# One head a step in stick-breaking, index projections later, a sixteenth weight slot, in a two-block transformer kernel

## The chip, the cores and the metric

The kernel runs on one core of a Trainium2 chip. The metric is the device time of one execution in microseconds. The engines are TensorE (PE), VectorE (DVE), ScalarE (ACT), GpSimd (POOL) and SyncE (SP, which issues most transfers). Each has its own program, written out by hand; semaphores join them.

## The reference

Two transformer blocks on 512 tokens of 1024 features in float32. Block one has two layers. Its first layer mixes with eight heads of "fox" attention (softmax with a cumulative forget gate) and eight heads of DSA (a small index score picks the keys), its second with NSA; each is followed by an MLP. Block two has four heads of differential attention, eight heads of stick-breaking attention, and a mixture of 32 experts. The parts that the change touches, cut down:

```python
def dsa_mixer(...):                       # block one, layer one
    q_abs = einsum('bshe,rhe->bshr', q[..., ROPE_DIM:], w_uk)
    rel = relu(einsum('bqhd,bsd->bqhs', qi, k_idx))      # index score
    score = einsum('bqhs,bqh->bqs', rel, wi)
    ...                                   # top 128 keys, softmax over them
    return einsum('bshr,rhd->bshd', o_lat, w_uv)

def fox_mixer(q, k, v, f_logit):
    cum = cumsum(log_sigmoid(f_logit))
    logits = q @ k.T * scale + cum_q - cum_k
    ...

def stick_breaking(q, k, v):              # block two, 8 heads of 64
    z = q @ k.T * scale
    log_1m = where(causal, log_sigmoid(-z), 0.0)
    between = cumsum(log_1m, reverse=True) - log_1m
    a = where(causal, exp(log_sigmoid(z) + between), 0.0)
    return a @ v                          # then rms_norm per head, then w_o

def hier_moe(h, ...):                     # top 2 of 8 experts in the top group
    for each expert e:
        ys = (silu(xb @ w1[e]) * (xb @ w3[e])) @ w2[e]
    return sum over the two experts of gate * ys
```

## The kernel before

Activations lie transposed, features on the 128 partitions and the 512 tokens along the free dimension. Dense layers go through `pe_block`, a scheme of seven products instead of eight on two blocks at a time, with six weight tiles in a ring. Two PSUM banks (`ch6`, `ch7`) are channels for small results: PE fills one, ACT or DVE takes it to SBUF (`act_take`, `dve_take`), and PE waits until it has been emptied. The stages come one after another, and four of them matter here.

**Preparation, index and soft steps (block one).** `pe_ab_prepare` rotates and turns queries and keys. At its end it projects the shared latent (`ck`, two tiles) to the DSA keys (`k_dsa`, four tiles, L627 and L628) and values (`v_dsa`, four tiles, L633). `dve_ab_prepare` forms the forget gates' cumulative sums, takes half of those tiles, and builds the operands `fls` and `frs` that add a gate to the logits (L1657 to L1663). Then `pe_index` computes the index scores (L653), which DVE adds up (L1681). After it run sixteen fox steps and sixteen DSA steps, each a pair of heads and a block of 128 queries (`pe_soft`), software-pipelined over PE, ACT and DVE. SP brings the gates' rows into `frs` and `fls` by sixteen small transfers, and writes the rows of the relative-position bias out (`row`), while the soft steps run.

**Stick-breaking (block two).** `pe_sb`, `act_sb` and `dve_sb` run over four pairs of heads. The score matrix of a head is kept by key blocks j, so that block j has the 512 - 128 j queries at or after it; `PARTS` lists the eight blocks of a pair:

```python
PARTS = [(a, j, T - P * j) for a in range(2) for j in range(NB - 1, -1, -1)]
```

For each block PE forms logits (L974), ACT scales them out of PSUM (L1356), DVE masks the diagonal (L1976) and forms -|z| (L1981), ACT takes exp and ln(1 + .) (L1361, L1366), DVE adds max(z, 0) (L1996). So softplus(z) is there. PE sums it over later keys with a triangular and a ones matrix (L984, L986), DVE subtracts (L1985), ACT takes exp (L1370), and PE forms the values with the weights stationary (L994, twenty matmuls of 64 columns for a pair; the trace records each matmul of the program as two, so x40). DVE takes these, PE turns them (L1000), ACT takes them again. The banks are reused within a pair, and no pair begins its later sums before its logits are done. When all pairs are done, eight tiles `u` are normalised (`pe_norm_tiles` L881, `act_norm_tiles` L1071, L1079 and L1081, `dve_norm_tiles` L1921), and the output projection 2O begins.

**Experts.** 32 experts of six weight pieces of 1 MiB each. SP issues the 192 loads in the order `ORDER` into `SLOTS` = 15 places (L2150); a place is free when PE has used its piece (`w_used`). Eight of the places are free before the dense layers end, since the others lie over tiles that are still in use:

```python
if g == SLOTS - LATE:
    sp.wait_ge(s["prod_done"], 7 * N_CH // 2)
```

Each expert handles up to 64 tokens: POOL gathers them from `h_tokens` and scatters the result into `y_pairs`, DVE forms the indices (`dve_slots`, `dve_indices`) two experts ahead, PE runs the up matmuls (L2285) and the down matmuls (L2293). The last three experts are added by PE and DVE without going through memory (`pe_last` L2354, `dve_last` L2506). At the end SP loads the four blocks of `y_pairs` (1 MiB each, L2184), DVE adds them to the tokens `xtok` (L2491, L2493), and four transfers write the output. `pe_tokens` turns `x` into `xtok` around expert 0.

## Time and profile before

| what | value |
|---|---|
| median of 3 runs | 2469.31 us (2463.83 to 2474.63) |
| the profiled execution, its own time | 2470.12 us |
| its span | 2468.7 us |
| PE busy | 2286.4 us, 93% |
| DVE busy | 1391.5 us, 56% |
| ACT busy | 566.9 us, 23% |
| POOL busy | 65.9 us, 3% |
| data moved | 350.18 MB |

The span is the part of an execution between the first and the last recorded instruction; the own time of the same execution is 1.4 us longer. Busy shares are means over stages that have different limits, so each stage has to be read by itself. A row of a stretch gives start and end, its length, then for PE, PE's weight loads, DVE, ACT and POOL the busy time and the number of instructions, then PE's granted clock (1.00 is 2.4 GHz, 0.50 is 1.2 GHz), the DMA engines' busy share and GB/s.

### The profile page before, as it was taken

How to read it: one execution, taken by the hardware profiler on the slowest of the kernel's cores; microseconds unless marked ns; L12 is line 12 of the kernel's file. 1: busy time of each engine (PE TensorE's matmuls, PEld its weight loads, DVE VectorE, ACT ScalarE, POOL GpSimd, SP SyncE). 2: the span in 40 equal slices, each digit the busy share in tenths (PEclk: the TensorE clock that was granted, in tenths of full speed). 3: DMA queues.
4: the chain of work that ended last, by engine and by line, in shares of the span. 5: the costliest groups of instructions: out<-in, count | busy, mean ns of one | idle time of the engine just before them, and what ended most of it. 6: DMA issues, size and time to landing. Idle time of an engine off the chain costs nothing.

```text
span 2468.7 us, 29460 instructions
## 1 busy us (share of the span) xinstructions
PE 2286.4 (93%) x10906; PEld 1674.5 (68%) x10906; DVE 1391.5 (56%) x3563; ACT 566.9 (23%) x1397; POOL 65.9 (3%) x67
## 2 busy tenths in 40 slices
PE   8987889999999988999999999999889899898887
PEld 6863668888888876557888888887566733333332
DVE  6558857666566555997665666765756411111114
ACT  2013342101001013773110011202554211211111
POOL 0000000000000000000000000000000011111110
PEclk9998799999999986999999999999799898999999
DMA  5320022222222420001222332322003699999996
GB/s 204 92 60 7 11 75 83 88 86 86 86 86 86 157 69 0 1 2 52 86 86 92 90 91 86 103 86 68 1 1 130 243 388 419 419 419 419 420 420 279
DMA packets 69455, 350.18 MB, mean 142 GB/s; under 512 B 10804, under 2 KB 11060, under 8 KB 43776
## 3 DMA queue, kind: packets, MB, share of 16 engines
q1 hardware_dynamic: 64144, 339.18, 37.4%
q0 software_dynamic: 4880, 8.05, 0.9%
q8 instruction: 89, 1.46, 0.3%
q10 hardware_dynamic: 288, 1.05, 0.1%
q14 instruction: 54, 0.44, 0.1%
HBM read 343.05 MB, written 17.30 MB: 146 GB/s over the span
## 4 chain that ended last, share of the span: by engine, by line
PE 68%; DVE 7%; DMA 7%; ACT 3%; issue 2%; SPq 0%; DVEq 0%; POOLq 0%; ACTq 0%
PE bank L550 25%; PE bank L563 7%; PE bank L553 7%; PE bank L558 7%; DMA w<-in_experts 6%; PE bank L2285 6%; PE bank L2293 4%; PE bank L541 2%; DVE exps L1695 1%; PE bank L767 1%; PE bank L2261 1%; PE bank L812 1%; PE bank L837 1%; DMA y_pairs<-oN,idx 1%; PE bank L825 1%
## 5 line engine op out<-in xcount | busy, mean ns | idle before, releaser
L2285 PE MATMUL bank<-w,xT 128*64 128x512 f32 x1024 | 228.3, 594 | 8.1 <-DMA w<-in_experts 7.4
L2464 DVE COPY square<-bank 128x256 f32<-128x256 f32 x32 | 13.6, 425 | 356.8 <-ACT rope L2384 356.8
L2285 PEld LDWEIGHTS bank<-w,xT 128*64 128x64 f32 x1024 | 71.6, 137 | 159.9 <-issue 134.1
L1220 ACT ACTIVATE exps<-exps,small 128x128 f32<-128x128 f32 (+1 forms) x224 | 124.4, 559 | 99.0 <-DVE small L1695 98.4
L550 PE MATMUL bank<-u,ring 128*128 128x256 f32 x608 | 143.6, 379 | 0.0
L1471 DVE TENSOR_TENSOR third<-first,bank 128x256 f32<-128x256 f32 x108 | 45.5, 421 | 173.3 <-PE bank L550 172.6
L2293 PE MATMUL bank<-w,square 128*64 128x512 f32 x512 | 138.6, 691 | 2.1 <-ACT square L2391 2.1
L550 PEld LDWEIGHTS bank<-u,ring 128*128 128x128 f32 x608 | 115.5, 190 | 15.7
L550 PE MATMUL bank<-h_sums,w_sum 128*128 128x256 f32 x512 | 120.9, 379 | 0.0
L550 PE MATMUL bank<-h,ring 128*128 128x256 f32 x512 | 120.9, 379 | 0.0
L550 PE MATMUL bank<-u_mlp,ring 128*128 128x256 f32 x480 | 113.4, 379 | 0.0
L550 PE MATMUL bank<-u_mlp_sums,w_sum 128*128 128x256 f32 x480 | 113.4, 379 | 0.0
L550 PE MATMUL bank<-exps,w_sum 128*128 128x256 f32 x464 | 109.6, 379 | 0.0
L550 PEld LDWEIGHTS bank<-h_sums,w_sum 128*128 128x128 f32 x512 | 97.3, 190 | 13.2
L550 PEld LDWEIGHTS bank<-h,ring 128*128 128x128 f32 x512 | 97.3, 190 | 13.2
L1159 ACT ACTIVATE h<-relu 128x512 f32<-128x512 f32 x64 | 40.3, 630 | 273.7 <-DVE relu L1603 249.2
L550 PEld LDWEIGHTS bank<-u_mlp,ring 128*128 128x128 f32 x480 | 91.2, 190 | 12.4
L550 PEld LDWEIGHTS bank<-u_mlp_sums,w_sum 128*128 128x128 f32 x480 | 91.2, 190 | 12.4
L550 PEld LDWEIGHTS bank<-exps,w_sum 128*128 128x128 f32 x464 | 88.2, 190 | 12.0
L2293 PEld LDWEIGHTS bank<-w,square 128*64 128x64 f32 x512 | 38.9, 156 | 74.4 <-issue 70.7
L553 PE MATMUL bank<-u,ring 128*128 128x256 f32 x352 | 83.2, 379 | 0.0
L563 PE MATMUL bank<-u,w_sum 128*128 128x256 f32 x352 | 83.2, 379 | 0.0
(445 smaller groups left out, 4215.5 us busy)
## 6 DMA issues: line engine op xcount, KB each, us to landing
w<-in_experts SPq DMA_DIRECT2D x192, 1024.0 KB, 26.5
ring<-in_dense SPq DMA_DIRECT2D x216, 512.0 KB, 4.2
w<-y_pairs SPq DMA_DIRECT2D x4, 1024.0 KB, 26.6
consts<-in_consts SPq DMA_DIRECT2D x1, 2054.5 KB, 16.6
x<-in_xT SPq DMA_DIRECT2D x4, 512.0 KB, 7.4
cmp_v<-in_cmp_v SPq DMA_DIRECT2D x1, 2048.0 KB, 8.6
cmp_k<-in_cmp_k SPq DMA_DIRECT2D x1, 2048.0 KB, 13.0
h_tokens<-u SPq DMA_DIRECT2D x4, 512.0 KB, 3.9
```

The lines of the kernel that those rows point to most:

```text
L541: ins = pe.matmul(bank, w[:, j, :], x(j), start=i == 0, stop=i == 3)
L550: ins = pe.matmul(bank, w[:, j, :], x(j), start=j == 0, stop=j == 3)
L553: ins = pe.matmul(part[2], a12[:, j, :], tile(2 * j + 1)[:, 0:HT], start=j == 0, stop=j == 3)
L558: ins = pe.matmul(part[4], a22[:, j, :], t4[:, j, :], start=j == 0, stop=j == 3)
L563: ins = pe.matmul(part[3], s4[:, j, :], tile(2 * j + 1)[:, HT:T], start=j == 0, stop=j == 3)
L767: ins = pe.matmul(ch.bank[:, 0:64], k.cw1[n][:, l, :], k.xg[n][:, l, :, :].rearrange("p a n -> p (a n)"), start=l == 0, stop=l == CMP_LEN - 1)
L812: pe.matmul(logits_bank(k, n, a)[:, 0:P * (b + 1)], k.yc[r, m, b * P:(b + 1) * P], k.yc[r, (KS, KW)[x], 0:P * (b + 1)], start=True, stop=T ...
L1159: act.activation(k.hs[q % 2][:, j + a, :], k.rc[a], ACT.Square).then_inc(s["h_ready"], 1)
L1220: act.activation(e, e, ACT.Exp, bias=neg[:, a:a + 1], scale=-1.0, accum_out=total[:, a:a + 1]).then_inc(s[done], 1)
L1471: dve.tensor_tensor(u3, u2, part[7], ALU.add).then_inc(s["shared"], 1)
L2285: ins = k.pe.matmul(bank[a * CAP:(a + 1) * CAP, :], xT[:, kk % 4, kk // 4, :], w[:, (2 * (kk % 2) + a) * EH:(2 * (kk % 2) + a + 1) * EH], ...
L2293: ins = k.pe.matmul(bank[a * CAP:(a + 1) * CAP, :], hT[:, c % 2, c // 2, :], w[:, c % 2 * D + a * T:c % 2 * D + (a + 1) * T], start=c == 0 ...
```

## The change

1. *Preparation, index, soft steps.* The four `k_dsa` and four `v_dsa` projections leave `pe_ab_prepare`. Two `k_dsa` stand ahead of the second and third quarter of `pe_index`; two more are in soft steps 4 and 8, and the four `v_dsa` in soft steps 2, 6, 10 and 14. ACT takes them all. The gate operands are built by three memsets, before the copy of the causal tables, and the matmul that adds the gate has 2 rows instead of 64. `w_uk` is loaded later, into dead tiles. ACT takes a `row` first in its step rather than last.
2. *Stick-breaking.* A step is one head. Logits of head n, later sums of head n-1 and the values of a finished pair are in one step, on four sets of `z` and two of `plus`; a head's four blocks are three groups (512 columns, 384 + 128, 256). The scale is folded into the queries. Softplus is ln(1 + exp(min(z, 30))), then the maximum with z. The values are formed with v stationary (64 columns) and the weights moving, both heads of a pair into halves of one bank, so they come out turned. Each of the eight tiles of the norm has its place in the steps.
3. *Experts.* The constant tables that are dead by then form a further place for weights: `SLOTS` is 16, nine of them before the dense layers end. Slots and indices are formed three experts ahead. `x` is turned to tokens in experts 4 to 7.
4. *End.* The four loads of `y_pairs` are issued before the last two weight pieces, and DVE adds them before it adds the last expert.

```diff
-SLOTS = 15
+SLOTS = 16
...
-        k.wuk = k.et
-        k.wuv = k.on2
+        k.wuk = [k.m1, k.u3]
+        k.wuv = sb("w_uv", [P, 2, T], stack=st)
...
-    for m in range(4):
-        ch = k.channels[(m + 1) % 2]
-        pe.wait_ge(ch.emptied, ch.n)
-        for r in range(2):
-            pe.matmul(ch.bank, k.wuk[:, r, m * P:(m + 1) * P], ck[r], start=r == 0, stop=False)
-        ch.end(pe.matmul(ch.bank, k.const("sel_rope"), mi, start=False, stop=True), ("k_dsa", m))
...
+        if m in (1, 2):
+            pe_k_dsa(k, m - 1)
...
+        if m in (1, 2) and at == 0:
+            pe_k_dsa(k, m + 1)
+        if m < 4 and at == 2:
+            pe_v_dsa(k, m)
...
+SB_AT = {0: (0, 0), 1: (1, 0), 3: (1, 3 * P), 2: (2, 0)}
+SB_BLOCKS = ((0,), (1, 3), (2,))
+SB_IN, SB_BACK = (1, 2, 0), (2, 1, 0)
+SB_HEADS = 8
+SP_MOST = 30.0
+O_SQUARE = (0, 1, 2, 3, 4, 5, 7, 9)
+SB_STEPS = O_SQUARE[-1] + 2
...
+    for step in range(SB_STEPS):
+        if step < SB_HEADS:
+            pe_sb_logits(k, step)
+        if 0 <= step - 1 < SB_HEADS:
+            pe_sb_later(k, step - 1)
+        if step - 1 in O_SQUARE:
+            pe_o_norm(k, O_SQUARE.index(step - 1))
+        if step >= 3 and step % 2 and step - 2 < SB_HEADS:
+            pe_sb_values(k, (step - 3) // 2)
...
+def pe_sb_values(k, m):
+    pe, s, ch = k.pe, k.s, k.ch6
+    pe.wait_ge(s["a_ready"], 3 * (2 * m + 2))
+    pe.wait_ge(ch.emptied, ch.n)
+    for j in range(NB):
+        for a in range(2):
+            ins = pe.matmul(ch.bank[a * HD:(a + 1) * HD, j * P:T], k.vsb[:, j, m * P + a * HD:m * P + (a + 1) * HD],
+                            sb_block(k.z[(2 * m + a) % 4], j), start=j == 0, stop=j == 3)
...
+def act_sb_logs(k, n):
...
+    for g in (1, 0):
+        act.wait_ge(s["z_done"], 3 * n + SB_IN.index(g) + 1)
+        act.copy(k.z[n % 4][g], k.bank[g]).then_inc(s["z_read"], 1)
...
+    for step in range(SB_STEPS):
+        head, back = step < SB_HEADS, 0 <= step - 1 < SB_HEADS
+        if head:
+            dve_sb_least(k, step)
+        if back:
+            dve_sb_less(k, step - 1, 0)
+        if head:
+            dve_sb_plus(k, step, 0)
+            dve_sb_plus(k, step, 1)
+        if back:
+            dve_sb_less(k, step - 1, 1)
+        if head:
+            dve_sb_plus(k, step, 2)
+        if back:
+            dve_sb_less(k, step - 1, 2)
+        if step - 2 in O_SQUARE:
+            dve_o_norm(k, O_SQUARE.index(step - 2))
...
+PAIRS_AT = len(ORDER) - 2
+TURN = {p: g + (NB if g >= PAIRS_AT else 0) for g, p in enumerate(ORDER)}
...
+        if g == PAIRS_AT:
+            sync_pairs(k)
...
+AHEAD, X_TURN = 3, 4
...
     dve_last(k, NE - 2)
+    dve_pairs(k)
     dve_last(k, NE - 1)
-    dve_pairs(k)
```

The lines below are instructions in program order, before and after, each with its line number in the kernel that it belongs to. On PE, between the last rotations of the preparation (L594) and the index scores (L653), stood the projections of `k_dsa` (L627, L628) and `v_dsa` (L633):

```order
L594 MATMUL bank<-y_ab,consts 128x512
L627 MATMUL bank<-y_ab,expsT 128x512 x2
L628 MATMUL bank<-y_ab,consts 128x512
L627 MATMUL bank<-y_ab,expsT 128x512 x2
L628 MATMUL bank<-y_ab,consts 128x512
L627 MATMUL bank<-y_ab,expsT 128x512 x2
L628 MATMUL bank<-y_ab,consts 128x512
L627 MATMUL bank<-y_ab,expsT 128x512 x2
L628 MATMUL bank<-y_ab,consts 128x512
L633 MATMUL bank<-o_tokens,y_ab 128x512 x8
L594 MATMUL bank<-y_ab,consts 128x512
L653 MATMUL bank<-y_ab 128x256 x2
L653 MATMUL bank<-y_ab 128x384 x2
```

After the change PE goes from the rotations (now L598) to the index scores (now L665), with one `k_dsa` (L634, L635; `first` and `third` are the dead tiles that hold `w_uk`) ahead of the second quarter:

```order
L598 MATMUL bank<-y_ab,consts 128x512 x2
L665 MATMUL bank<-k_dsa,y_ab 128x256 x2
L665 MATMUL bank<-k_dsa,y_ab 128x384 x2
L665 MATMUL bank<-k_dsa,y_ab 128x512 x2
L634 MATMUL bank<-y_ab,first_26 128x512
L634 MATMUL bank<-y_ab,third_28 128x512
L635 MATMUL bank<-y_ab,consts 128x512
L598 MATMUL bank<-y_ab,consts 128x512
L665 MATMUL bank<-k_dsa,y_ab 128x256 x2
```

So twenty matmuls ahead of the first index score are gone, and three of them stand behind its first quarter.

On PE in the middle of stick-breaking, the last blocks' later sums (L984, L986) of a pair were followed by its values (L994), their turning (L1000) and then the logits of the next pair (L974):

```order
L984 MATMUL bank<-y_65,consts 128x512
L986 MATMUL bank<-y_65,consts 128x384
L986 MATMUL bank<-y_65,consts 128x256
L986 MATMUL bank<-y_65,consts 128x128
L994 MATMUL bank<-v_sb,y_65 128x64 x20
L1000 MATMUL bank<-consts,o_tokens 128x128 x4
L974 MATMUL bank<-y_65 128x128
L974 MATMUL bank<-y_65 128x256
L974 MATMUL bank<-y_65 128x384
L974 MATMUL bank<-y_65 128x512
```

After the change, logits (L1025) and later sums (L1037, L1039) of two neighbouring heads stand in one step, then a tile of the norm (L902) and the values (L1049) of a finished pair:

```order
L1037 MATMUL bank<-y_66,consts 128x512
L1039 MATMUL bank<-y_66,consts 128x384
L1039 MATMUL bank<-y_66,consts 128x256
L1039 MATMUL bank<-y_66,consts 128x128
L902 MATMUL bank<-square_7,consts 128x512
L1049 MATMUL bank<-y_66,v_sb 64x512 x2
L1049 MATMUL bank<-y_66,v_sb 64x384 x2
L1049 MATMUL bank<-y_66,v_sb 64x256 x2
L1049 MATMUL bank<-y_66,v_sb 64x128 x2
L1025 MATMUL bank<-y_66 128x384
L1025 MATMUL bank<-y_66 128x128
L1025 MATMUL bank<-y_66 128x256
```

The values' twenty matmuls of 64 columns and four transposes became eight wide ones, and the norm's matmul stands among the steps.

On SP at the end of the experts' loads, the weight pieces (L2150) were followed by the four blocks of pairs (L2184):

```order
L2150 DMA w_74<-in_experts 128x2048
L2150 DMA w_75<-in_experts 128x2048
L2150 DMA w_76<-in_experts 128x2048
L2184 DMA w_77<-y_pairs 128x2048
L2184 DMA w_78<-y_pairs 128x2048
L2184 DMA w_79<-y_pairs 128x2048
L2184 DMA w_80<-y_pairs 128x2048
```

Now the pairs (L2284) stand ahead of the last two pieces (L2243):

```order
L2243 DMA w_77<-in_experts 128x2048
L2243 DMA w_78<-in_experts 128x2048
L2284 DMA w_79<-y_pairs 128x2048
L2284 DMA w_80<-y_pairs 128x2048
L2284 DMA w_81<-y_pairs 128x2048
L2284 DMA w_82<-y_pairs 128x2048
L2243 DMA w_83<-in_experts 128x2048
L2243 DMA w_84<-in_experts 128x2048
```

The last two pieces moved behind four transfers of the same size.

## Rows read from the trace of the kernel before

**Rows 1.** Busy time by stage, columns as in the section on the profile:
```profile
194.90:218.00 23.10, 16.24 (x54) 6.75 (x54) 22.02 (x40) 10.75 (x24) 0.00 (x0) 0.85 0.02 2
218.00:306.00 88.00, 72.79 (x358) 49.16 (x358) 81.79 (x268) 28.20 (x88) 0.00 (x0) 0.77 0.03 12
...
1777.10:1868.40 91.30, 82.85 (x401) 59.19 (x400) 52.58 (x136) 53.62 (x133) 0.00 (x0) 0.91 0.00 1
1868.40:1882.90 14.50, 10.24 (x16) 3.15 (x17) 8.22 (x16) 12.60 (x23) 0.00 (x0) 0.88 0.00 1
```

**Rows 2.** Timeline ahead of the index scores: start, length, engine, line:
```profile
176.67 1.96 PE L627 MATMUL bank<-y_ab,expsT 128*128 128x512 f32 x4
...
180.50 0.41 DVE L1650 TENSOR_SCALAR w_sum<-w_sum 8x512 f32<-8x512 f32 x1
...
187.04 7.03 PE L633 MATMUL bank<-o_tokens,y_ab 128*128 128x512 f32 x16
...
194.72 0.89 DVE L1657 COPY y_ab<-consts 128x256 f32<-128x256 f32 x3
...
199.89 0.68 DVE L1617 TENSOR_TENSOR rope<-y_ab,consts 128x512 f32<-128x512 f32 x1
```

**Rows 3.** DVE's waits in the fox steps, and two stretches there:
```profile
DVE expsT L1759 <- PE bank L737: 4.1, 4, 1.8
...
255.05:257.90 2.85, 0.47 (x4) 0.42 (x4) 2.81 (x10) 2.23 (x6) 0.00 (x0) 1.00 0.00 0
260.75:263.60 2.85, 2.85 (x15) 2.65 (x16) 1.06 (x3) 0.59 (x2) 0.00 (x0) 0.50 0.00 0
```

**Rows 4.** Groups by line and shape in stick-breaking: busy us, mean ns | idle before:
```profile
L1976 DVE TENSOR_TENSOR y<-y,consts 128x128 f32<-128x128 f32 x32 | 9.3, 290 | 12.4 <-ACT y L1356 12.1
...
L1985 DVE TENSOR_TENSOR y<-y,bank 128x512 f32<-128x512 f32 x8 | 5.5, 684 | 6.4 <-PE bank L986 6.4
L1361 ACT ACTIVATE y<-y 128x512 f32<-128x512 f32 x8 | 5.0, 630 | 1.8 <-DVE y L1981 1.8
...
L1356 ACT ACTIVATE y<-bank 128x512 f32<-128x512 f32 x8 | 4.6, 580 | 0.7 <-PE bank L974 0.7
...
L1361 ACT ACTIVATE y<-y 128x256 f32<-128x256 f32 x8 | 3.3, 416 | 0.3
```

**Rows 5.** The chain of waits, values of the first pair:
```profile
1795.70 4.43 PE bank L994 x40
```

**Rows 6.** Timeline of PE in later sums, and DVE with a scalar operand:
```profile
1793.38 1.02 PE L984 MATMUL bank<-y,consts 128*128 128x512 f32 x2
1794.24 1.46 PE L986 MATMUL bank<-y,consts 128*128 128x384 f32 x6
...
1737.14 0.49 DVE L1964 TENSOR_SCALAR exps<-exps,small 128x512 f32<-128x512 f32 x1
```

**Rows 7.** Groups by line in the norm of eight tiles:
```profile
L1071 ACT ACTIVATE square<-u 128x512 f32<-128x512 f32 x8 | 4.8, 615 | 0.0
L1079 ACT ACTIVATE norm_root<-bank,eps 128x512 f32<-128x512 f32 x7 | 4.7, 671 | 1.6 <-PE bank L881 1.6
```

**Rows 8.** Stretches before and after the first expert's start, and of the experts:
```profile
1917.00:1932.00 15.00, 15.00 (x75) 13.28 (x73) 6.67 (x16) 3.59 (x7) 0.00 (x0) 1.00 0.03 10
...
1964.50:1974.00 9.50, 7.84 (x49) 3.93 (x44) 2.57 (x10) 2.18 (x6) 0.00 (x0) 1.00 0.90 347
2000.00:2434.00 434.00, 385.16 (x1808) 149.22 (x1809) 78.02 (x287) 74.94 (x169) 57.00 (x56) 0.95 1.01 419
```

**Rows 9.** The end: DVE's timeline, and the loads of `y_pairs`:
```profile
2451.48 4.87 DVE L2506 TENSOR_TENSOR u<-u,bank 128x512 f32<-128x512 f32 x8 [4.39 <-PE bank L2354]
...
2464.82 1.22 DVE L2493 TENSOR_TENSOR u<-u,w 128x1024 f32<-128x1024 f32 x1
...
L2184 SPq DMA_DIRECT2D w<-y_pairs x4: 326/1982/2135, 2418.3 to 2422.7; - x4
...
DMA to landing us min/median/max: 6.7/26.3/27.2
```

More of the change, by code:

```diff
@@ new lines, in pe_sb_logits, with pe_sb_later @@
+def pe_sb_logits(k, n):
+    pe, s, y = k.pe, k.s, k.y2
+    m, a = divmod(n, 2)
+    r = slice(a * HD, (a + 1) * HD)
+    for g in SB_IN:
+        if n and g == 2:
+            pe.wait_ge(s["z_read_w"], n)
+        elif n:
+            pe.wait_ge(s["z_read"], 2 * n if g == 0 else 2 * n - 1)
+        for j in SB_BLOCKS[g]:
+            ins = pe.matmul(sb_block(k.bank, j), y[r, SK + m, j * P:(j + 1) * P], y[r, SQ + m, j * P:T], start=True, stop=True)
+        ins.then_inc(s["z_done"], 1)
+def pe_sb_later(k, n):
+    pe, s = k.pe, k.s
+    sp, banks = k.plus[n % 2], k.bank[3:6]
+    for i, g in enumerate(SB_BACK):
+        pe.wait_ge(s["sp_ready"], 3 * n + (3 if g == 0 else 2))
+        if n:
+            pe.wait_ge(s["z_less"], 3 * (n - 1) + i + 1)
+        for j in SB_BLOCKS[g]:
+            ins = pe.matmul(sb_block(banks, j), k.const("tri_from"), sb_block(sp, j), start=True, stop=j == 3)
+            for jj in range(j + 1, NB):
+                ins = pe.matmul(sb_block(banks, j, jj), k.const("ones"), sb_block(sp, jj), start=False, stop=jj == 3)
+        ins.then_inc(s["later_done"], 1)
@@ L1226, in act_soft @@
         m, at = divmod(step, 4)
+        if 1 <= m <= 4 and at == 0:
+            act_take(k, k.ch7, ("row", m - 1, 1), k.row[m - 1][:, T:LV], k.ch7.bank[:, 0:LV - T])
+        if m in (1, 2) and at == 1:
+            act_take(k, k.ch7, ("k_dsa", m + 1), k.kd[:, m + 1, :], k.ch7.bank)
+        if m < 4 and at == 3:
+            act_take(k, k.ch7, ("v_dsa", m), k.vd[:, m, :], k.ch7.bank)
         if step < len(SOFT):
@@ L2206, in moe_tensor @@
     pe.wait_ge(s["h_copied1"], NB)
-    pe_meta(k, 0)
-    pe_meta(k, 1)
-    pe_tokens(k, (0, 1))
+    for e in range(AHEAD):
+        pe_meta(k, e)
     pe_x_turn(k, 0)
@@ L2453, in moe_vector @@
     dve_route(k)
-    dve_slots(k, 0)
-    dve_indices(k, 0)
-    dve_slots(k, 1)
-    dve_indices(k, 1)
+    for e in range(AHEAD):
+        dve_slots(k, e)
+        dve_indices(k, e)
     dve_count(k)
```

393 lines of the change are left out of this document (190 added, 203 removed).

## The prediction

> **What bounds the kernel now.** I read the busy time by stage first, since the whole program is one stage after another and only in the experts do stages overlap with loads. PE is busy for 93% of the span, but a stage is worth only what its own limit allows. In the index scores DVE is busy 22.0 of 23.1 us and in the fox steps 81.8 of 88.0, while PE has 6.9 and 15.2 us to spare there [rows 1]: DVE is the limit. In stick-breaking no engine is full: 91.3 us, of which PE is busy 82.9, ACT 53.6 and DVE 52.6; the norm after it, 14.5 us, is ACT's (12.6 busy) [rows 1]. So these 105.8 us are bound by engines that wait for each other in turn, and the groups of stick-breaking show it: DVE's mask sits idle 12.4 us for ACT's scaling, DVE's subtraction 6.4 us for PE's sums [rows 4], and a pair's values hold the chain of waits for 4.43 us with nothing of the next pair beside them [rows 5]. The experts are bound by transfers once these flow; before they flow, 15 us of the output projection have a DMA share of 0.03 [rows 8]. At the end DVE works alone: the last expert's sums and then the pairs [rows 9].
>
> **Part A, preparation, index and soft steps.** Ahead of the index scores PE runs the k_dsa projections from 176.67 on and the v_dsa projections from 187.04 for 7.03 us [rows 2]. They are 10.37 and 7.03 us, 2.6 and 1.8 us each, and DVE's rotation for the scores starts at 199.89, after it took four of these tiles and built the gate operands [rows 2]. Without them, DVE is through with the gate sums at 180.91 (180.50 and 0.41) and has the copies of 0.89 [rows 2] and three memsets of 512 columns ahead, at the 0.49 of another one-input operation of that size [rows 6], and some 0.5 of steps between them, an estimate: 180.9 + 0.9 + 1.5 + 0.5 = 183.8. That is 16.1 us sooner. Of the projections, two of 2.6 us come into the index scores, where PE's 6.9 idle us hide them in the sum, and two of 2.6 and four of 1.8, 12.4 us in all, into the fox steps. PE's 15.2 idle us there would hide these if they fell in the right places. But PE's clock is 0.50 in some stretches: in 255.05 to 257.90 PE was busy 0.47 us, and by 260.75 it ran at 0.50 and full, and DVE already waits 1.8 us once for the turned weights, 4.1 us in four waits [rows 3]. So a projection there may cost twice its 2.6, or nothing. Between nothing and the full 12.4 I take 6, about half, since no row is nearer to either end. DVE's own work in these steps is unchanged, and ACT's six more takes at about 0.6 [rows 4] disappear in its 28.2 busy of 88 [rows 1]. The sixteen gate transfers hide behind the index scores; if that cover were gone, the first fox step would wait for them. The 2-row gate matmul has the same columns as the one of 64 rows, so I cost it at nothing; the row taken first in its step frees a channel sooner, also nothing. **A = -16.1 + 6 = -10**, bounds -4 (12.4 back) and -16.
>
> **Part B, stick-breaking and its norm.** The work per head of 64 features, by engine. One head has 512 + 384 + 256 + 128 = 1280 columns of logits, and a ones or triangular matmul of 512 columns takes 0.86 us (1793.38 to 1794.24) [rows 6]. PE: logits 2.15, later sums 2560 columns 4.3, one norm tile 0.86, and values: 2560 columns for a pair. With both heads in halves of the array at once they take 2.15 a pair, 1.1 a head; one after the other 2.15 a head, which is near the 4.43 a pair of before [rows 5]. I take 1.1: 8.4 us a head. ACT: two copies out of PSUM at 0.58, exp of 512, 512 and 256 columns at 0.63, 0.63 and 0.42 [rows 4], ln and the last exp about the same, 6.2 in all; a square 0.62, a root of two calls of about 0.67 [rows 7], and half a take of 0.6: 8.4. DVE is lower (masks four at 0.29, min three at up to 0.49 [rows 6], maximum and subtraction three each at up to 0.68, a gain): about 8.
>
> The three are close, so what counts is the loop between them. ACT's program for a step is copies, exps and lns of head n, then the last exp of head n-1, which waits for DVE's last subtraction, which stands behind DVE's last maximum of head n. So a round is: copy 0.58, two masks 0.58, min 0.49, exps and lns 3.3, maximum 0.68, subtraction 0.69, exp 0.63 = 6.95 [rows 4, 6]. To it ACT adds the take 0.3, the root 1.3 and the square 0.6: **9.2 us a head**, against 11.4 a head of before (91.3 over eight). PE's 8.4 fits below it, since logits of head n+1 need only ACT's and DVE's reads of head n and its later sums run beside ACT's lns.
>
> The sum: the first head 8.3 (6.95 and its first logits), steps 1 to 5 with a norm tile each 46.0, steps 6 and 7 with fewer of them 8.6 and 8.2, then what is left of the last head's later sums and weights 2.0, its values 2.2, take 0.6, square 0.6, norm matmul with its way 1.0, root 1.3, gain 0.75 and the sums that follow 0.8. Together 80.4 us in place of 105.8: **B = -25**. If the handoffs keep a head at the 11.4 of before, seven steps give back 15 us and it is -10; if they cost nothing above the busiest engine's 8.4, it is -30. Two small edits cost nothing: the scale in the queries is the same operation with a scalar, and fewer, wider blocks are counted above.
>
> The Trainium skill (TensorEngine Tiling (Array Packing), Key Properties) says that changing the tiling mode drains TensorE first. By it each of the four groups of value matmuls costs a drain before and one after, and at the half of a 0.86 us matmul for each the total would be 2431 instead of 2428. No row here shows a gap to price it by, and the sum leaves it out.
>
> **Part C, experts and end.** One more MiB before the dense layers end: the stretch of 15 us with DMA share 0.03 takes one piece more [rows 8]. At 419 GB/s, the rate in the experts [rows 8], 1 MiB is 2.5 us, and the last load ends that much sooner, **-2.5**. In the stretch behind the first expert's start (1964.50 to 1974.00) PE is busy 7.84 of 9.5 and the DMA share is 0.90, not full [rows 8]; the token transposes there move away, and with them a tenth of 9.5: **-1.0**. PE is idle more before the first expert without the transposes; for a lower clock there I add 1.0, an estimate of the same size, so that the two cancel. In experts 4 to 7 the transposes lie beside transfers that bound the stage, so cost nothing. At the end, DVE was through with the sums of expert 30 at 2447.1 (2451.48 less its idle 4.39), waited for PE, ran the last sums for 4.87, and then the pairs until 2466.04, eight adds in 9.7 from 2456.3; the last output took 2.7 to the end of the span at 2468.7 [rows 9]. Now the pairs, which landed up to 27 us after issues at 2418.3 to 2422.7 [rows 9], land four places, two pieces, sooner, and DVE adds them in the time in which it waited: 2447.1 + 9.7 + 4.9 + 2.7 = 2464.4, which is **-4.3**. The last two pieces are then the last to land, at about 2449.9 (2422.7 + 27.2) [rows 9]; half of the down matmuls, the take and the first sums make PE ready for DVE some 4 us later, at 2453.9, before DVE asks at 2456.8, so that is hidden with 2.9 to spare. What SP waits for ahead of the pairs, expert 28's scatter, came at about the first issue, 2418.3; transfers still queued cover it by some 20 us. **C = -2.5 - 4.3 = -7**, bounds -4 and -10.
>
> **The sum.** 2470.1 (own time of the profiled execution, 0.8 above the median of the runs shown) - 10 - 25 - 7 = **2428 us**. With all bounds at once it ends at 2470 - 18 = 2452 and 2470 - 56 = 2414.
>
> **The rivals.** (1) The handoffs in stick-breaking stay as they were, 11.4 a head: for it speaks that before no engine was full there either [rows 1]; against it that heads now overlap. B = -10, total **2443**. (2) The projections come back in full in the fox steps and something more waits with them, A between 0 and -4: for it speaks the half clock and the wait in rows 3. Total **2436**. (3) The 16th place and the reordered end give nothing, because the last pieces, ten us later in the queue, hold PE and with it DVE past 2456.8: C = 0, total **2435**. (4) The other side: PE in stick-breaking falls to 1.2 GHz. Before, a PE busy for 0.47 of 2.85 us was followed by a clock of 0.50 [rows 3]; PE has short fills between its groups in the new steps too. All at 1.2 GHz PE needs 16.8 us a head, 8 x 16.8 + 9 = 143 for 105.8, +38, so with A and C 2470 + 38 - 17 = **2491**. The kernel is slower from the point at which B is +17, that is at a step of 15.0 us (122.8 less 17.6, over seven), which needs PE cold for about 80% of its work. Before, at a like load, the clock was 0.91 over the stage [rows 1]; in the new steps PE is busy 8.4 of 9.2. The Trainium skill (TensorE: Matmul & The Clock Gate, Part 1) has a cold clock as the default and makes steady activity release it; the trace agrees in that the stretch at 0.50 followed one with PE nearly idle.
>
> **Chances and range.** The forecast's own case (B within -18 to -30, A and C within their bounds) 0.62; rival 1 0.20; rival 2 0.08; rival 3 0.07; rival 4 or a like loss 0.02; nothing changes 0.01. All but the last two end faster. A measurement tells about 0.5%, 12.3 us, from no change, and 2452 is 17 us below before: faster 0.96, same 0.02, slower 0.02. The ends 2414 and 2452 need every bound at once. For 8 in 10 I take 2414 to 2446, which holds rivals 1 to 3; the upper side is longer because of rival 1.
>
> **What would show it.** Right: DVE's first rotation for the scores some 16 us sooner than 199.89; fox steps longer by some 6 us, with PE named in DVE's waits at steps 4 and 8; stick-breaking with its norm about 80 us long, at 9 to 9.5 us a head with ACT's exp waiting for DVE's subtraction; the output projection behind it with no norm stage between; DVE's pair adds ahead of its last sums and the end about 3 us after those. Wrong: a head at 11 us or more; the fox steps 12 us longer; PE idle in the last experts behind the last two pieces; a PE clock of 0.5 over whole steps of stick-breaking.

## The result

The changed kernel takes 2434.41 us, the median of four runs (2432.66 to 2435.18), and the kernel before, on the same chip, 2469.02 us. The ratio is 0.9858, with a 95% interval from 0.9836 to 0.9881, so 35 us less. The prediction was 2428, its range 2414 to 2446. Later the same program was measured once more beside the experiments, in another session: 2431.56 us of 2473.86, ratio 0.9817 (0.9788 to 0.9846), 45 us less by the ratio. The two intervals overlap; what lies between them is told below.

By stage the profiled execution (own time 2434.59, span 2433.3) reads as follows. These are the stretches of the changed kernel, with the same columns as the rows of the kernel before: the index scores from DVE's first rotation, the soft steps, stick-breaking with its norm up to the first matmul of 2O, and from there to the end.

```profile
184.35:204.67 20.32, 15.56 (x64) 7.21 (x64) 19.55 (x34) 9.23 (x20) 0.00 (x0) 0.97 0.02 2
204.67:362.86 158.19, 140.53 (x741) 93.65 (x740) 113.66 (x395) 59.88 (x181) 0.00 (x0) 0.82 0.10 36
1773.95:1853.23 79.28, 76.79 (x306) 45.71 (x306) 53.76 (x131) 59.05 (x115) 0.00 (x0) 0.92 0.00 1
1853.23:2433.30 580.07, 507.64 (x2409) 234.90 (x2407) 150.16 (x478) 107.22 (x234) 64.03 (x61) 0.94 0.92 378
```

And the two middle stretches in the kernel before, cut in the same way:

```profile
220.20:367.82 147.62, 124.56 (x713) 91.26 (x711) 113.73 (x395) 56.48 (x175) 0.00 (x0) 0.82 0.11 38
1777.18:1882.92 105.74, 93.03 (x418) 62.34 (x418) 60.82 (x152) 66.24 (x155) 0.00 (x0) 0.90 0.00 1
```

| stage | before | after | change | forecast |
|---|---|---|---|---|
| up to the first rotation for the scores | 199.89 | 184.35 | -15.5 | -16.1 |
| index scores | 20.3 | 20.3 | 0 | 0 |
| soft steps | 147.6 | 158.2 | +10.6 | +6 |
| first output projection to the end of differential attention (unchanged) | 1409.4 | 1411.1 | +1.7 | 0 |
| stick-breaking and norm | 105.7 | 79.3 | -26.5 | -25 |
| 2O to the end | 585.8 | 580.1 | -5.7 | -7 |
| span | 2468.7 | 2433.3 | -35.4 | -42 |

The stages agree in kind with the forecast; the largest single miss is in the soft steps. The row without a change has a spread of its own: the same part of the program took 1405.2 to 1411.2 us in the profiles of this document. Here is why DVE took longer in the soft steps, in the timeline of PE in the fifth fox step. The k_dsa projection stands in it at half clock:

```profile
222.13 2.08 PE L634 MATMUL bank<-y_ab,first 128*128 128x512 f32 x2 [0.35 <-ACT y_ab L1130]
224.00 1.92 PE L634 MATMUL bank<-y_ab,third 128*128 128x512 f32 x2
225.70 1.91 PE L635 MATMUL bank<-y_ab,consts 128*128 128x512 f32 x2
```

The three matmuls run from 222.13 to 227.4, some 5.3 us, where 2.6 is their cost at full clock. The turns behind them reach DVE late. That is the row of DVE at the end of it, and the sum of such waits in the fox steps of this kernel:

```profile
229.16 0.56 DVE L1812 COPY expsT<-bank 128x384 f32<-128x384 f32 x1 [4.48 <-PE bank L759]
```
```profile
DVE expsT L1812 <- PE bank L759: 12.2, 5, 5.9
```

The second row covers 222 to 300; over the whole of the fox steps (202 to 291) it is 11.7 us in four waits. Before, that wait was 4.1 us in four [rows 3]. The longest here, 5.9 us, is longer than the whole of it.

In stick-breaking the chip shows another limit than the forecast named. These are two stretches of nine us out of the middle of it:

```profile
1802.00:1811.00 9.00, 9.00 (x44) 5.07 (x43) 7.51 (x19) 7.44 (x16) 0.00 (x0) 1.00 0.00 0
...
1829.00:1838.00 9.00, 9.00 (x39) 5.81 (x38) 6.87 (x19) 6.87 (x14) 0.00 (x0) 1.00 0.00 0
```

PE is busy all the time, DVE and ACT are not. And in PE's timeline there, from the norm's matmul of one step to that of the next:

```profile
1822.31 1.02 PE L902 MATMUL bank<-square,consts 128*128 128x512 f32 x2
1823.26 2.37 PE L1049 MATMUL bank<-y,v_sb 128*64 128x512 f32 x16
1825.57 2.42 PE L1025 MATMUL bank<-y 64*128 64x384 f32 x8
1827.92 0.70 PE L1037 MATMUL bank<-y,consts 128*128 128x256 f32 x2
...
1831.06 1.46 PE L1039 MATMUL bank<-y,consts 128*128 128x384 f32 x6
1832.36 1.02 PE L902 MATMUL bank<-square,consts 128*128 128x512 f32 x2
1833.31 0.91 PE L1025 MATMUL bank<-y 64*128 64x384 f32 x2
```

The values of two heads take 2.31 us (1823.26 to 1825.57), near the 2.15 of both in halves of the array at once and far from the 4.3 of one after the other. From one head's first logits (1825.57) to the next head's (1833.31) it is 7.74 us in a step without values; with values 10.05. The mean is 8.9 us a head. The forecast had 8.4 for PE and 9.2 for the loop.

At the end DVE adds the pairs ahead of the last sums, without a gap, as forecast; the last output lands 4.5 us after the last sum (2428.81 to the end of the span at 2433.3):

```profile
2409.34 4.87 DVE L2607 TENSOR_TENSOR u<-u,bank 128x512 f32<-128x512 f32 x8 [5.41 <-PE bank L2455]
2414.24 1.23 DVE L2590 TENSOR_TENSOR u<-u,w 128x1024 f32<-128x1024 f32 x1
2415.46 5.33 PE L2397 MATMUL bank<-w,square 128*64 128x512 f32 x16 [2.47 <-DMA w<-in_experts]
...
2422.69 1.22 DVE L2592 TENSOR_TENSOR u<-u,w 128x1024 f32<-128x1024 f32 x1
...
2423.94 4.87 DVE L2607 TENSOR_TENSOR u<-u,bank 128x512 f32<-128x512 f32 x8
2425.26 2.73 SPq L2800 DMA_DIRECT2D out<-u  x2
```

### The profile page after: what moved, and what is told of

The parts are those of the page before. It is cut to its first block, busy times and chain, and to the rows that moved or that the text cites. A ratio compares the mean times of both kernels' runs of the same rounds, so it can differ in the third digit from the quotient of the medians.

```text
span 2433.3 us, 29180 instructions
## 1 busy us (share of the span) xinstructions
PE 2272.5 (93%) x10794; PEld 1655.0 (68%) x10794; DVE 1377.7 (57%) x3531; ACT 560.9 (23%) x1361; POOL 67.8 (3%) x67
## 4 chain that ended last, share of the span: by engine, by line
PE 72%; DVE 7%; DMA 4%; ACT 2%; issue 1%; SPq 0%; DVEq 0%; ACTq 0%
PE bank L554 25%; PE bank L2389 8%; PE bank L567 7%; PE bank L557 7%; PE bank L562 7%; PE bank L2397 4%; DMA w<-in_experts 4%; PE bank L545 2%; PE bank L2362 1%; DVE exps L1748 1%; PE bank L789 1%; PE bank L834 1%; PE bank L847 1%; DVE square L2532 1%; PE bank L1037 1%
## 5 line engine op out<-in xcount | busy, mean ns | idle before, releaser
L2389 PE MATMUL bank<-w,xT 128*64 128x512 f32 x960 | 216.2, 598 | 7.5 <-DMA w<-in_experts 6.8
L1522 DVE TENSOR_TENSOR third<-first,bank 128x256 f32<-128x256 f32 x108 | 45.4, 421 | 173.1 <-PE bank L554 172.4
L2397 PE MATMUL bank<-w,square 128*64 128x512 f32 x480 | 127.5, 678 | 5.5 <-ACT square L2491 2.9
L554 PEld LDWEIGHTS bank<-h,ring 128*128 128x128 f32 x512 | 97.3, 190 | 13.2
L554 PEld LDWEIGHTS bank<-h_sums,w_sum 128*128 128x128 f32 x512 | 97.3, 190 | 13.2
L554 PEld LDWEIGHTS bank<-u_mlp_sums,w_sum 128*128 128x128 f32 x480 | 91.2, 190 | 12.4
L554 PEld LDWEIGHTS bank<-u_mlp,ring 128*128 128x128 f32 x480 | 91.2, 190 | 12.4
```

The costliest lines, as they stand in the source:

```text
L554: ins = pe.matmul(bank, w[:, j, :], x(j), start=j == 0, stop=j == 3)
L1522: dve.tensor_tensor(u3, u2, part[7], ALU.add).then_inc(s["shared"], 1)
L2389: ins = k.pe.matmul(bank[a * CAP:(a + 1) * CAP, :], xT[:, kk % 4, kk // 4, :], w[:, (2 * (kk % 2) + a) * EH:(2 * (kk % 2) + a + 1) * EH], ...
L2397: ins = k.pe.matmul(bank[a * CAP:(a + 1) * CAP, :], hT[:, c % 2, c // 2, :], w[:, c % 2 * D + a * T:c % 2 * D + (a + 1) * T], start=c == 0 ...
```

## The experiments

The first three are each one part of the change, applied to the kernel before. In what follows "2O to the end" is from the first matmul of the output projection 2O to the end of the span.

### Part A alone

```diff
+def pe_k_dsa(k, m):
...
+        if m in (1, 2) and at == 0:
+            pe_k_dsa(k, m + 1)
+        if m < 4 and at == 2:
+            pe_v_dsa(k, m)
...
+    for rows in k.frs:
+        own.link(dve.memset(rows, 1.0))
+    dve.memset(k.fls, 1.0).then_inc(s["cum_ready"], 1)
```

Expected: 

> The kernel before with part A alone (projections moved, gate operands by memsets, 2-row gate matmul). Theory, from the traces of before and after: DVE's first rotation for the scores 15.5 us sooner, soft steps 4 and 8 give back about 4 us each and later steps 2 more, so the output projection starts 5 us sooner and the whole is about 5 us shorter. Rival, the forecast's sum: 10 us shorter.

Measured: 2467.64 us of 2474.86, ratio 0.9965 (0.9942 to 0.9988), 8.7 us less by the ratio. In the profiled execution the soft steps begin at 202.91 and end at 357.41, 154.5 us after 147.6 of before. The first rotation comes at 182.59, 17.3 us sooner. So the part gives back 6.9 us in the soft steps, and 10.4 us are left at their end, which is the rival's 10 and not the theory's 5. The ratio's 8.7 lies between the two, and its interval (3 to 14 us) holds both. The twelve runs spread from 2452.55 to 2473.68, which neither had: five lie at 2452.6 to 2458.4 with a mean granted clock of 0.958 to 0.964, seven at 2464.7 to 2473.7 with 0.945 to 0.952. The profile is of one of the five.

### Part B alone

```diff
+SB_STEPS = O_SQUARE[-1] + 2
...
-    pe_norm_tiles(k, "o2", ["ones"] * 4 + ["pair_ones"] * 4)
...
+    for step in range(SB_STEPS):
+        if step < SB_HEADS:
+            pe_sb_logits(k, step)
```

Expected: 

> The kernel before with part B alone (stick-breaking one head a step, norm inside). Theory: from the first logits to the first matmul of 2O 79 us instead of 105.7, and the whole 26 us shorter. Rival: part B is worth less alone, since the experts' loads are what ends last and their stream starts no sooner than the dense layers let it; then under 22.

Measured: 2447.8 us, ratio 0.9889 (0.9866 to 0.9912), 27 us less. From the first logits to 2O it took 79.25 us (1785.29 to 1864.54), the same as in the changed kernel. The term of B is what the theory says, and it arrives at the end in full. This execution shows something else too: its soft steps, where its program is that of before, took from 220.26 to 374.10, 153.8 us, against 147.6 in the kernel before.

### Part C alone

```diff
-SLOTS = 15
+SLOTS = 16
...
+PAIRS_AT = len(ORDER) - 2
...
+AHEAD, X_TURN = 3, 4
```

Expected: 

> The kernel before with part C alone (16th place, three experts ahead, tokens later, pairs before the last two pieces). Theory: 2O's start to the end 580 us instead of 585.8, the whole 6 us shorter, with the first expert's up matmuls at half clock (8.8 us instead of 7.1). Rival: with part A and B in place C costs or gains something else, so the three parts alone don't add to the 35 us of the whole.

Measured: 2468.61 us, ratio 0.9973 (0.9956 to 0.9991), 6.7 us less by the ratio; in the profiled execution 2O to the end is 582.75 us, 3.1 less than before. The three parts by their ratios add up to 43 us, the whole measured 35 and 45 in its two measurements. So the parts add, as far as these intervals can tell.

### All k_dsa in the index scores

```diff
-        if m in (1, 2):
+        if m in (1, 2, 3):
             pe_k_dsa(k, m - 1)
...
+    pe_k_dsa(k, 3)
...
-        if m in (1, 2) and at == 0:
-            pe_k_dsa(k, m + 1)
```

Expected: 

> The changed kernel with the k_dsa projections of soft steps 4 and 8 moved into the index scores (one ahead of the last quarter, one behind it). Theory: steps 4 and 8 lost 4.2 and 4.0 us because DVE waited there for PE at half clock; they give these back, the end of the index scores costs 1 to 2, so 6 us shorter than the changed kernel, soft steps 5 to 15 offset by 15 us from before instead of 7 to 11. Rival: the loss is PE's work itself wherever it stands in this stretch (or the clock's phase), and the soft steps end no sooner than in the changed kernel.

Measured: 2428.73 us of 2474.86, ratio 0.9811 (0.9787 to 0.9836). The index scores end no later (18.3 us from their first sum, as in the changed kernel), and the soft steps take 150.9 us (204.29 to 355.21) instead of 158.2. By the ratio the whole can't be told from the repeat of the changed kernel (0.9817), so the argument rests on the profiles. DVE's wait in the fox steps is about half of the changed kernel's, in the same view:

```profile
DVE expsT L1810 <- PE bank L758: 6.3, 9, 1.5
```

The longest wait fell from 5.9 to 1.5 us. So the projections' place in steps 4 and 8 did cost time, as the theory says; and they cost nothing measurable inside and behind the index scores. Part of the 7.3 us is not theirs: of the kernels here that have the changed kernel's soft steps, three took 157.9 to 158.4 us in them, at a mean granted clock of 0.82 to 0.83, and five took 154.3 to 154.6, at 0.84 to 0.85. Against these five it is 3.4 to 3.7. The soft steps of this kernel stand in two later ones too, and took 150.7 and 150.8 us there.

### One more logits matmul a head, and one more ACT copy a step

The first makes one matmul twice:

```diff
-        for j in SB_BLOCKS[g]:
+        for j in SB_BLOCKS[g] + SB_BLOCKS[g][:g == 0]:
```

Expected: 

> The changed kernel with one more logits matmul of 512 columns a head (the first block's is made twice, with the same result). Theory, from the changed kernel's trace: in the steps with a norm tile PE has no idle time between 1802 and 1847, so it sets the pace at 8.9 us a head, and each head becomes 0.86 longer: from the first logits to 2O 79.3 + 6.5 = 86. Rival, the forecast's: the loop of ACT and DVE sets 9.2 a head and PE's 8.4 + 0.86 still fits beside it, so at most 1 us longer.

Measured, in one execution: 85.11 us from the first logits to 2O. A head takes 8.60 or 10.91 us instead of 7.74 or 10.05, 0.86 more each, which is the matmul in full (the first ten us were at 0.67 here, at 0.50 in the 79.3):

```profile
1771.83:1856.94 85.11, 81.86 (x321) 47.58 (x321) 54.06 (x131) 59.86 (x115) 0.00 (x0) 0.94 0.00 1
```

The second adds to ACT:

```diff
+            more = k.act_own.link(k.act.copy(k.ET[0], k.vsb[:, 0, :]))
```

Expected: 

> The changed kernel with one more ACT copy of 512 columns (0.58 us, of a tile that nobody reads) in each step of stick-breaking. Theory, PE sets the pace and ACT is idle some 1.4 us a step: at most 1.5 us longer than 79.3 (first ten us at a clock of 0.50) or 74.8 (at 1.00). Rival, the forecast's loop over ACT and DVE: each of some eight steps 0.58 longer, 4.6 in all.

Measured, in one execution: 78.26 us, with the clock at 1.00 at the start, so 3.5 more than 74.8. The steady heads still take 7.74 and 10.05, one of them 10.42; from the last head's first logits to 2O it takes 23.38 instead of 20.3. The first numbers speak for the theory, the total for neither: the extra copies cost next to nothing while PE sets the pace, and 3.1 us in the last head's steps. PE's timeline says where. By the last head ACT is late enough that PE waits 0.77 us for DVE, which stands behind ACT's ln, and behind that wait the granted clock is 0.64 for 4.8 us. In the kernel with 15 places, with the same steps and no extra copy, PE doesn't wait there, and the clock is 1.00 (last two rows):

```profile
1820.40 1.03 PE L1037 MATMUL bank<-y,consts 128*128 128x256 f32 x2 [0.77 <-DVE y L2067]
...
1820.40:1825.20 4.80, 4.80 (x14) 3.38 (x15) 2.44 (x5) 3.94 (x9) 0.00 (x0) 0.64 0.00 0
```
```profile
1823.96 0.70 PE L1037 MATMUL bank<-y,consts 128*128 128x256 f32 x2
1821.60:1828.50 6.90, 6.90 (x31) 4.53 (x30) 4.85 (x13) 5.38 (x11) 0.00 (x0) 1.00 0.00 0
```

From the logits to the sums behind them it is 3.19 us instead of 2.35, and from these sums to the values 6.21 instead of 4.53: 2.5 of the 3.1 us. The rest is 0.2 behind the values and 0.4 at the last norm tile, whose wait for ACT's square grew from 1.35 to 1.73. So ACT and DVE with 0.58 us more a head are about as slow as PE, and the room between the two is small.

### Two experts ahead again

```diff
-AHEAD, X_TURN = 3, 4
+AHEAD, X_TURN = 2, 4
```

Expected: 

> The changed kernel with slots and indices two experts ahead again (tokens still turned in experts 4 to 7). Theory: the third expert's slots and indices delay the first expert by 3.4 us, so 2O to the first up matmul is 77.4 instead of 80.8 us, the stream of loads restarts that much sooner, and 2O to the end is 3 us shorter than the 580.1 of the changed kernel. Rival: three ahead keeps the gathers off the path later, so the stream of loads runs dry somewhere and the gain is lost; 580 or more.

Measured: 2425.8 us of 2474.34, ratio 0.9795 (0.9754 to 0.9836), no slower than the changed kernel as a whole. In the profiled execution 2O to the first up matmul is 80.23 us against 80.8, and 2O to the end 586.8. The theory's 3.4 us did not come. In the first 60 us of the experts the loads moved 317 GB/s, in the repeat of the changed kernel 359:

```profile
1920.61:1980.61 60.00, 54.10 (x206) 20.10 (x206) 9.20 (x36) 8.95 (x21) 6.03 (x6) 0.78 0.85 317
```
```profile
1934.53:1994.53 60.00, 53.60 (x224) 20.85 (x226) 10.41 (x40) 8.95 (x21) 7.18 (x7) 0.84 0.92 359
```

That is what the rival says: the stream runs thin in the first experts. But PE's clock is 0.78 in the one and 0.84 in the other, and the whole kernel was not slower. The kernel before also works two ahead, and in its first 60 us, at a clock of 0.97, it moved 362 GB/s:

```profile
1962.58:2022.58 60.00, 53.91 (x270) 22.21 (x272) 10.29 (x40) 11.70 (x26) 8.09 (x8) 0.97 0.93 362
```

The changed kernel's first profile, at 0.94, moved 371. So two ahead alone doesn't thin the stream, the clock is as good a reading, and what three ahead is worth stays open.

### Pairs last again

```diff
-PAIRS_AT = len(ORDER) - 2
+PAIRS_AT = len(ORDER)
...
-    dve_pairs(k)
     dve_last(k, NE - 1)
+    dve_pairs(k)
```

Expected: 

> The changed kernel with the loads of pairs behind the last two weight pieces and DVE's adds of them behind its last sums, as before. Theory: from the last landing to the end 18.8 instead of 15.5 us, so 2O to the end 583.4 us, 3.3 longer. Rival, the forecast's term: 4.3 longer. Rival two: the end is set by the last landing alone and nothing changes.

Measured: 2434.79 us of 2474.34, ratio 0.9837 (0.98 to 0.9874), which can't be told from the changed kernel. In the profiled execution the last landing to the end takes 17.7 us, and 2O to the end 586.4, that is 2.4 to 6.3 more than in the changed kernel's two executions (584.0 and 580.1). The sign is that of the theory and the first rival; for the size one execution is too few. One thing this execution does show, how the outputs leave. Behind the pairs' adds they leave 2.4 us apart again (DVE's two adds of 1.22 stand between them), and the last lands 2.7 us after DVE's last add (2421.06 to 2423.7):

```profile
2413.90 5.13 SPq L2798 DMA_DIRECT2D out<-u  x2
2419.83 1.23 DVE L2592 TENSOR_TENSOR u<-u,w 128x1024 f32<-128x1024 f32 x1
```

### 15 places

```diff
-SLOTS = 16
+SLOTS = 15
...
-    k.w = {j: k.sb(f"w{j}", [P, PIECE]) for j in late + list(range(SLOTS - LATE - 1))}
-    done = k.cpack.at["swap"][0]
-    k.w[SLOTS - LATE - 1] = k.consts[:, done:done + PIECE]
+    k.w = {j: k.sb(f"w{j}", [P, PIECE]) for j in late + list(range(SLOTS - LATE))}
```

Expected: 

> The changed kernel with 15 places for weights again. Theory: the DMA engines are idle before the dense layers end, so one piece less there lets the stream end 2.5 us later, 2O to the end 2.5 longer (581.2 on the mean of three runs, so 583.7). Rival: the places fill up in the first experts anyway, which wait for gathers and not for weights, and it makes no difference.

Measured: 2432.06 us of 2473.86, ratio 0.9838 (0.9808 to 0.9868), against 0.9817 for the changed kernel in the same session; 2O to the end 584.5 us. Both the theory and its rival stay possible: the difference expected, 2.5 us, is within the spread of that stretch (580.1 and 584.0 with the same program).

### The changed kernel again

Nothing is changed in it.

Expected: 

> The changed kernel once more, beside the others on one chip. Theory: its spread comes from the clock that PE is granted in stretches where PE waits; from the first logits to 2O it takes 79.3 us where the first ten us are at 0.50 and 74.8 where they are at 1.00, with the same program. Rival: the two lengths belong to the variants in which they were seen (74.8 in the two with other experts, 79.3 in this one), and it takes 79.3 again whatever the clock.

Measured: 2431.56 us, six runs of which three are shorter and three longer, 2422.9, 2423.3 and 2426.2 us with a mean granted clock of 0.957 to 0.960, and 2436.9, 2439.0 and 2440.6 us with 0.951 to 0.955. The profiled one is of the longer three: stick-breaking takes 79.25 us, and its clock in the first ten us is 0.50. The 15-place kernel has the same program there and took 74.80 us. These are the first ten us of each, first of the changed kernel (its first profile), then of the 15-place kernel with the whole stage:

```profile
1773.95:1783.95 10.00, 9.44 (x22) 5.63 (x22) 5.13 (x15) 5.97 (x13) 0.00 (x0) 0.50 0.00 0
```
```profile
1767.10:1777.10 10.00, 8.71 (x36) 5.66 (x36) 7.13 (x21) 8.08 (x17) 0.00 (x0) 1.00 0.00 0
1767.10:1841.90 74.80, 71.27 (x305) 42.48 (x305) 53.54 (x131) 59.08 (x115) 0.00 (x0) 1.00 0.00 1
```

At 0.50 PE is busy 9.44 us with 22 matmuls, at 1.00 it does 36 in 8.71. From the first head's logits to the third's it is 16.0 us and 11.2; all steady heads agree to 0.01 us. The rival (that the length belongs to the variant) isn't ruled out by the repeat alone, since it was at 0.50 both times; the clock column explains both lengths. What decides the clock at the start is another question, and the last run below tries one answer.

### Two better versions

The first has all k_dsa in the index scores, and of the pairs' loads two ahead of the last two pieces and two behind; DVE adds the first two before the sums of expert 30.

```diff
+PAIR_TURN = (PAIRS_AT, PAIRS_AT + 1, PAIRS_AT + 4, PAIRS_AT + 5)
...
+    dve_pairs(k, (0, 1))
     dve_last(k, NE - 2)
-    dve_pairs(k)
+    dve_pairs(k, (2, 3))
     dve_last(k, NE - 1)
```

Expected: 

> The changed kernel with all k_dsa projections in the index scores, and with two of the four loads of pairs ahead of the last two weight pieces and two behind, DVE adding the first two before the sums of expert 30. Theory: soft steps 4 and 8 give back their 3 to 4 us each less 1 to 2, so 5 us shorter than the changed kernel in the soft steps; at the end DVE waits 5.4 us before the sums of expert 30 in the changed kernel and now adds there, 3 us shorter. Together 8 us faster than the changed kernel. Rivals: the soft steps' time comes from the clock's state and not from these projections, then only 3 us; the output's transfers or the last landing sets the end, then nothing at the end.

Measured: 2425.86 us of 2473.86, ratio 0.9789 (0.9765 to 0.9812), 5.7 us below the changed kernel's median of the same session. The intervals still overlap. The soft steps take 150.7 us, 7.6 less than in the repeat (158.35), and 3.6 to 3.9 less than in the five shorter profiles of those steps. From the last landing to the end it is 13.2 us instead of 15.6, 2.4 less where 3 were expected; but 2O to the end is 584.1 us, as in the repeat (584.0), so the gain at the end doesn't arrive in the stage as a whole.

The second is the same with four more matmuls at the end of differential attention, whose results nobody reads:

```diff
+        else:
+            k.pe.wait_ge(k.s["d_masked"], 2 * len(DA))
+            k.pe.matmul(k.bank[0], k.const("ones"), k.vda[:, 0, :], start=True, stop=True)
```

Expected: 

> The kernel of best1 with four more matmuls of 512 columns that nobody reads, one in each of the last four steps of differential attention, where PE waits for DVE 0.4 to 1.6 us a time. Theory: PE's clock at the start of stick-breaking follows how much PE idled just before; with the gaps filled it starts at 1.00 and from the first logits to 2O it takes 74.8 instead of 79.3 us, for at most 1.5 us later start; the median falls 2 to 3 us below best1's, since some executions were at 1.00 anyway. Rival: the clock falls by something else (the phase in which the chip looks), the profiled run again shows 0.50 and 79.3, and the four matmuls only cost up to 3 us.

Measured: 2415.9 us of 2472.87, ratio 0.9769 (0.9746 to 0.9792). Its five runs lie between 2413.19 and 2418.78. The first ten us of stick-breaking are at 0.83, and the stage takes 76.09 us, where the version without the four matmuls was at 0.50 and took 79.27:

```profile
1759.74:1769.74 10.00, 8.71 (x30) 5.89 (x30) 7.13 (x21) 8.09 (x17) 0.00 (x0) 0.83 0.00 0
```
```profile
1762.82:1772.82 10.00, 9.43 (x22) 5.64 (x22) 5.13 (x15) 5.97 (x13) 0.00 (x0) 0.50 0.01 2
```

The last six us before it have a clock of 1.00 with PE busy throughout. But the kernel with all k_dsa in the index scores, which has none of the four matmuls, shows the same first ten us and 75.99 us for the stage:

```profile
1762.38:1772.38 10.00, 8.72 (x30) 5.75 (x30) 7.13 (x21) 8.08 (x17) 0.00 (x0) 0.83 0.01 2
```

In both, the stage's first five us are at 1.00, and matmuls take twice as long only behind PE's first wait for DVE, of 1.0 us. And three profiles without the four matmuls have 1.00 in all ten. So that the clock followed the four matmuls is not shown. Nor is the gain of the whole: the ratios 0.9769 and 0.9789 of the two versions have intervals that overlap, from different sessions.

## Why the prediction was right, point by point

**Part A: right in kind; the size of its give-back depends on the execution.** The rotation came at 184.35 where 183.8 was forecast. The step "between nothing and the full 12.4 I take 6" gave 10.6 and 10.7 us in the two profiles of the changed kernel and 10.3 in the one with a further logits matmul, but 6.7 to 7.0 in five others with the same soft steps. All these are counted from the 147.6 us of before, and those steps too took 153.8 us in one execution. So 6 was near the commoner length, and half of the miss of the first comparison is the length that the changed kernel happened to have. The forecast said where, steps 4 and 8, and that twice the 2.6 was possible: the timeline shows 5.3 us there at half clock, and DVE's waits in these two steps are 4.48 and 5.88 us where they were 0.20 and 1.79. The kernel with all k_dsa in the index scores shows that moving the two away takes back at least 3.4 us. So the half was near as a sum and not as a mechanism: the cost sits in the steps in which DVE already waited for PE, and moving the two away took back 3.4 to 7.3 us, that is 1.7 to 3.7 for each projection of 2.6. The argument for index time, PE's idle 6.9 us there, was right, even for four projections.

**Part B: right in size, wrong in what sets the pace, and helped by luck.** The forecast was 80.4 us, measured 79.3. "PE's 8.4 fits below it" failed: PE needs 8.9 a head and is never idle in the steady heads, since each of its terms is longer than summed (logits 2.35 for 2.15, later sums 4.44 for 4.3, the norm tile 0.95 for 0.86, the values 1.16 for 1.1). The loop over ACT and DVE, put at 9.2, is shorter than that: with 0.58 more on ACT five heads grew by 0.4 us together, with 0.86 more on PE each grew by 0.86. The sum came out since the two paces lie 0.3 us apart, and since misses on single pieces cancelled. The first two heads took 16.0 us where 17.5 were summed, the next five 43.3 for 45.4, and from the last head's first logits to 2O it took 19.9 for 17.5. The last piece hides two larger misses. "What is left of the last head's later sums and weights 2.0" was 6.0 (1842.50 to 1848.54). And the last root, gain and sums, 2.85 us, were put ahead of 2O, which doesn't wait for them; it starts 0.97 us after the last norm matmul, as in the kernel before:

```profile
1842.50 0.70 PE L1037 MATMUL bank<-y,consts 128*128 128x256 f32 x2
...
1846.94 1.02 PE L902 MATMUL bank<-square,consts 128*128 128x512 f32 x2
1848.54 2.37 PE L1049 MATMUL bank<-y,v_sb 128*64 128x512 f32 x16 [0.58 <-ACT y L1423]
1852.26 1.12 PE L902 MATMUL bank<-square,consts 128*128 128x512 f32 x2 [1.35 <-ACT square L1112]
1853.23 0.59 PE L545 MATMUL bank<-u,ring 128*128 128x256 f32 x2
```

With the clock at 1.00 from the start the first two heads take 11.2 us and the stage 74.8, a clock effect that the sum doesn't have. The Trainium skill (TensorEngine Tiling (Array Packing), Key Properties) says that a change of the tiling mode drains TensorE. No run here changes the mode alone, but the trace bounds the cost: from the norm matmul's start to the values' it is 0.95 us where 0.86 is its own, and the values take 2.31 where 2.15 is theirs, so at most 0.25 us for both changes together and 1 us in all, not the 3 us weighed in the forecast.

**Part C: smaller than forecast.** 2O to the end was 585.8, 587.0 and 587.4 us in the three profiled kernels without part C, and in six with it 580.1, 580.9, 582.5, 582.8, 584.0 and 588.1, a mean of 583.1: 3.7 us less, where 7 were forecast. Against a spread of 8 us these means alone don't tell C from nothing; its own ratio does, 0.9973 (0.9956 to 0.9991). The single kernels with one piece of C undone can't settle its terms. What the trace shows at the end: DVE's order came as forecast (pairs from 2414.24, no wait before the last sums), but "the last output took 2.7" failed. Before, the four outputs left 2.4 us apart, behind two adds of 1.22 each [rows 9]; now they leave 1.2 us apart behind two sums of 0.6, and the last lands 4.5 us after the last sum instead of 2.7 (5.1 in the repeat). That is 1.8 of the 4.3 us, and it goes with the order: 3.9 to 5.1 us in the ten profiles with pairs ahead of the last sums, 2.7 in all four with pairs last, among them the changed kernel with pairs last again. At the start, 2O to the first up matmul grew from 79.7 to 80.8 us, and the first expert's up matmuls ran 8.8 us instead of 7.1, at a clock of 0.80 instead of 1.00; I had 1.0 for both, and it is 2.8. With two experts ahead again it is 80.2 and 8.8, so the third expert's slots are not what cost most of this.

**The rivals.** Rival 1, 11.4 us a head, is refuted. Rival 2 came close in the changed kernel's own profiles, where A ends at 5.0 and 4.6 us and the rival had 0 to 4; in part A alone it ends at 10.4. Rival 3 would have C at nothing: it gave 3.7 on the mean. Rival 4's mechanism does act, a low clock in stick-breaking, but only in the first 10 to 15 us, at a price of 4.5 us where 38 would be all of it. The Trainium skill (TensorE: Matmul & The Clock Gate, Part 1) has the low clock as the state of an idle engine. The traces agree in part: the steady heads, in which PE never idles, were at 1.00 in both profiles of the changed kernel. But its start at 0.50 came behind ten us in which PE was busy 6.7, and the start at 1.00 of the kernel with pairs last behind ten in which it was busy 6.4. What decides the start is open.

**The range.** The first measurement, 35 us less, and the repeat, 45 us less by the ratio, lie on both sides of the forecast's 42. By stage the misses of the first were +5 in A, -1.5 in B, +1.3 in C and +1.7 in a part without a change.

## What to carry to other kernels

Work that is put into an engine's idle time is free only where nobody already waits for that engine: in this case two projections of 2.6 us each cost 3.4 us at least in steps where DVE was waiting for PE, and nothing measurable in and behind a stage that another engine ends. When a software pipeline replaces a serial chain, add up every engine's work to the tenth of a microsecond, since the pace goes to the fullest one: 8.9 of PE beat a loop estimated at 9.2. Sum the last item of a pipeline by itself, and only up to the instruction that the next stage waits for; here that piece had misses of 4 and 3 us that hid each other. After moving adds ahead of the last step, look at how the outputs then leave together.

## What was not expected of the hardware

The same program has several lengths, and they go with PE's granted clock. The soft steps, with the program of before, took 147.6 us twice, at a mean clock of 0.82, and 153.8 us once, at 0.76. Stick-breaking took 79.25 to 79.28 us in four profiles with a clock of 0.50 in its first ten us, 76.0 and 76.1 in two with 0.83, and 74.78 to 74.80 in three with 1.00; the steady heads in all of them took 7.74 and 10.05. The changed kernel's six runs of one session were 2422.9 to 2440.6 us, with mean clocks of 0.960 to 0.951. This is larger than most single terms of the forecast, so such terms have to be read from stages at a like clock, and from more than one profile. A short wait can come ahead of a long low stretch: with one more ACT copy in stick-breaking, a wait of 0.77 us was followed by 4.8 us at a clock of 0.64. What sets the clock at a stage's start was not found; the four matmuls in PE's gaps were no test of it, since a kernel without them had the same 0.83.
